# VectorE's expert steps 2 to 13 as one hardware loop, with the first tile's closing norm moved behind the last step

## What is computed

```
v1, i1 = lax.top_k(s1, K)
v2, i2 = lax.top_k(s2, K)
cand_s = (v1[..., :, None] + v2[..., None, :]).reshape(B, T, H, K * K)
cand_e = (i1[..., :, None] * PEER_N_KEYS + i2[..., None, :]).reshape(B, T, H, K * K)
top_s, top_pos = lax.top_k(cand_s, K)
experts = jnp.take_along_axis(cand_e, top_pos, axis=-1)
g = jax.nn.softmax(top_s, axis=-1)
...
u = expert_down[e].astype(f32)
hdn = jax.nn.gelu(jnp.einsum('chkd,cd->chk', u, xt.astype(f32)))
return jnp.einsum('chk,chkd->cd', gt * hdn, expert_up[e].astype(f32))
...
h = h + peer_ffn(rms_norm(h, norm2_g[layer]), ...)
return rms_norm(h, norm_f_g)
```

## Time and profile before

| what | value |
|---|---|
| median of 3 runs | 871.92 us (871.73 to 872.32) |
| the profiled execution's own time | 871.49 us |
| its span in the profile | 869.8 us |
| busy: PE, DVE, ACT, POOL | 753.9, 563.8, 177.5, 580.4 us |
| gathers (queue q0) | 268.47 MB, 77.7% of 16 engines' span |
| HBM read | 306.93 MB |

### The profile page before, as it was taken

The page is one execution under the profiler, slowest core; times in us unless marked ns, Lnnn a source line. Parts: engine busy times, 40 slices in busy tenths (PEclk is TensorE's granted clock), DMA queues, the critical chain, the costliest instruction groups (busy, mean ns, idle before and its releaser), DMA issues.

```text
span 869.8 us, 9153 instructions
## 1 busy us (share of the span) xinstructions
PE 753.9 (87%) x2453; PEld 388.7 (45%) x2453; DVE 563.8 (65%) x1501; ACT 177.5 (20%) x557; POOL 580.4 (67%) x718
## 2 busy tenths in 40 slices
PE   8999999999997979788888888787878797777786
PEld 5988768556552424244333434242434342222232
DVE  2554686239998667676667676676666676765534
ACT  1134455211212021122202030203020211102010
POOL 5886551017777777777777777777777777777760
PEclk9999999999999999999999999999999999999999
DMA  8858460669999999999999999999999999999995
GB/s 291 224 149 221 156 253 2 233 250 359 398 410 383 411 408 410 410 410 409 409 409 409 409 409 410 409 410 408 410 409 410 410 409 410 409 410 411 410 409 230
DMA packets 99619, 308.94 MB, mean 355 GB/s; under 512 B 18512, under 2 KB 23424, under 8 KB 99584
## 3 DMA queue, kind: packets, MB, share of 16 engines
q0 software_dynamic: 73728, 268.47, 77.7%
q1 hardware_dynamic: 24784, 39.91, 13.8%
q10 hardware_dynamic: 1072, 0.16, 0.1%
HBM read 306.93 MB, written 1.05 MB: 354 GB/s over the span
## 4 chain that ended last, share of the span: by engine, by line
DMA 31%; PE 27%; POOL 23%; issue 11%; DVE 7%; ACT 1%; POOLq 0%; ACTq 0%; DVEq 0%
PE bank L1526 23%; DMA region_w<-in_expert_up,chosen 19%; POOL region_w L643 17%; DMA region_w<-in_expert_down,chosen 5%; DMA dn_spare<-in_expert_down,chosen 4%; POOL gates L643 3%; DMA pool_bd<-in_expert_down,chosen 3%; PE xn_ps L1526 2%; PE bank L1529 2%; DVE region_w L1382 2%; POOL pool_bd L643 1%; POOL dn_spare L643 1%; DVE gates L1382 1%; DVE pool_bd L1382 0%; DMA hvrep<-in_norm_g 0%
## 5 line engine op out<-in xcount | busy, mean ns | idle before, releaser
L1526 PE MATMUL bank<-region_w,pool_bd 128*128 128x512 f32 (+2 forms) x1004 | 472.6, 598 | 102.1 <-DMA region_w<-in_expert_up,chosen 99.8
L1526 PEld LDWEIGHTS bank<-region_w,pool_bd 128*128 128x128 f32 x1004 | 174.0, 189 | 372.7 <-issue 297.2
L643 POOL DMA_INDIRECT region_w<-in_expert_up,chosen x250 | 237.7, 951 | 81.3 <-issue 60.9
L1382 DVE CUSTOM_DVE_ANT_0 region_w<-xn_ps,region_w 128x1024 f32<-128x1024 f32 x128 | 156.5, 1224 | 101.4 <-DMA region_w<-in_expert_down,chosen 101.0
L643 POOL DMA_INDIRECT region_w<-in_expert_down,chosen x128 | 121.2, 947 | 40.5 <-issue 33.2
L1382 DVE CUSTOM_DVE_ANT_0 gates<-xn_ps,gates 128x1024 f32<-128x1024 f32 x64 | 78.1, 1223 | 36.2 <-DMA gates<-in_expert_down,chosen 34.1
L906 ACT ACTIVATE pool_bd<-ident,pool_bd 128x128 f32<-128x128 f32 x250 | 78.5, 389 | 80.7 <-PE bank L1526 59.8
L643 POOL DMA_INDIRECT gates<-in_expert_down,chosen x64 | 61.1, 955 | 23.4 <-issue 17.4
L709 ACT ACTIVATE pool_bd<-bank 128x256 f32<-128x256 f32 (+3 forms) x49 | 19.0, 389 | 267.1 <-PE bank L1526 242.9
L1382 DVE CUSTOM_DVE_ANT_0 dn_spare<-xn_ps,dn_spare 128x1024 f32<-128x1024 f32 x32 | 39.2, 1224 | 24.0 <-DMA dn_spare<-in_expert_down,chosen 23.9
L1526 PE MATMUL bank<-region_q,oT 128*128 (+1 forms) x240 | 54.3, 379 | 0.0
(11 more groups left out here) (285 smaller groups left out, 782.2 us busy)
## 6 DMA issues: line engine op xcount, KB each, us to landing
region_q<-in_w_in SPq DMA_DIRECT2D x4, 2048.0 KB, 8.8
region_q<-in_w_query SPq DMA_DIRECT2D x1, 6144.0 KB, 22.6
region_w<-in_expert_up,chosen POOLq DMA_INDIRECT x250, 14.4
region_w<-in_w_out SPq DMA_DIRECT2D x1, 3072.0 KB, 21.0
x_sb<-in_x SPq DMA_DIRECT2D x4, 512.0 KB, 4.1
region_q<-in_w_in SPq DMA_DIRECT2D x2, 1024.0 KB, 10.7
region_q<-in_w_in SPq DMA_DIRECT2D x16, 128.0 KB, 3.0
region_w<-in_wb_nsa SPq DMA_DIRECT2D x2, 1024.0 KB, 16.4
```

Of the source, the lines that this page charges most:

```text
L643: pool.indirect_dma_start(out=row, out_offset=None, in_=table, in_offset=bass.IndirectOffsetOnAxis(ap=of_slot(chosen, s, k), axis=0)).then ...
L1382: dve.tensor_tensor_reduce(out=row, in0=xn_ps[:, :], in1=row, scale=1.0, scalar=0.0, op0=ALU.mult, op1=ALU.add, accum_out=hdn[:, k:k + 1]) ...
L1526: return pe.matmul(out_, lhsT, rhs, start=start, stop=stop)
```

## The change

Three things are edited.

1. DVE: one loop runs turns 2 to 13. The number of the tile is now the loop's register shifted right by three, so the columns of `stat` (the per-token scales) are addressed by a register, and the wait for the second tile's tokens (`xn_in`) is in each turn, against a value worked out in a register. The wait for the scales (`rstd2`) in a turn is for 6 from the start, that is, for both tiles. The two `add_y(0, ...)` and `hy_ready` stand behind the loop, at step 14 in place of step 9, and `norm_f(0)` stands behind the coefficients of step 15.
2. ACT: its sum of squares moves from step 9 to step 13, behind that step's `softmax_exp`.
3. POOL: the 1/root moves from before up row 160 to before up row 240.

```diff
         def per_token(what, t):
-            return stat[:, what + t:what + t + 1]
+            return stat[:, bass.ds(what + t, 1)]
...
-                if n == 10 * SLOTS:
+                if n == LAST * SLOTS:
                     pool.wait_ge(ssq3, 1)
                     rstd(stat[:, 26:27], stat[:, 24:25], DM).then_inc(rstd3, 1)
...
-                if s == NH + 1:
-                    act.wait_ge(hy_ready, 1)
-                    act.activation(gt[:, 1, 0:DM], xs[:, 0, :], ACT.Square, accum_out=stat[:, 24:25]).then_inc(ssq3, 1)
                 if s + 2 < STEPS:
                     softmax_exp(s + 2)
...
+                if s == LAST - 2:
+                    act.wait_ge(hy_ready, 1)
+                    act.activation(gt[:, 1, 0:DM], xs[:, 0, :], ACT.Square, accum_out=stat[:, 24:25]).then_inc(ssq3, 1)
                 gelu_tanh(s + 1)
...
             def highest(p, t):
-                dve.wait_ge(rstd2, 3 * t + 3)
+                dve.wait_ge(rstd2, 6 if not isinstance(p, int) else 3 * t + 3)
...
-            def turn(s, t, t_next, t_choice):
-                picking = choose(s + 2, t_choice)
+            def turn(s):
+                picking = choose(s + 2, (s + 2) >> 3)
                 next(picking)
                 for k in range(SLOTS - AHEAD, SLOTS):
                     dot(k, s)
                     next(picking, None)
-                polynomial(s, t)
-                if t_next != t:
-                    dve.wait_ge(xn_in, 4)
-                begin(s + 1, t_next, picking)
+                polynomial(s, s >> 3)
+                dve.wait_ge(xn_in, 2 + 2 * ((s + 1) >> 3))
+                begin(s + 1, (s + 1) >> 3, picking)
...
-            turns(2, NH - 2, 0)
-            turn(NH - 2, 0, 0, 1)
-            turn(NH - 1, 0, 1, 1)
-            turn(NH, 1, 1, 1)
+            behind = own.n
+            with dve.Fori(2, LAST - 1) as i:
+                own.turn = (i - 2) * OWN_TURN
+                turn(i)
+            own.turn, own.n = 0, behind + OWN_TURN * (LAST - 3)
             dve.wait_ge(up_used, NH * SLOTS)
             own.mark(add_y(0, 0))
             own.mark(add_y(0, 1))
             own.wait()
             dve.engine_nop().then_inc(hy_ready, 1)
-            turns(NH + 1, LAST - 1, 1)
-            dve.wait_ge(gf_in, 16)
-            dve.wait_ge(rstd3, 1)
-            norm_f(0)
...
             polynomial(LAST, 1)
             coefficients(LAST)
+            dve.wait_ge(gf_in, 16)
+            dve.wait_ge(rstd3, 1)
+            norm_f(0)
```

More of the change, by code:

```diff
@@ L1465, in turn @@
                     next(picking, None)
-                polynomial(s, t)
-                if t_next != t:
-                    dve.wait_ge(xn_in, 4)
-                begin(s + 1, t_next, picking)
[L1471 to L1478, removed]
-            begin(2, 0, picking)
-            turns(2, NH - 2, 0)
-            turn(NH - 2, 0, 0, 1)
-            turn(NH - 1, 0, 1, 1)
-            turn(NH, 1, 1, 1)
+                polynomial(s, s >> 3)
+                dve.wait_ge(xn_in, 2 + 2 * ((s + 1) >> 3))
+                begin(s + 1, (s + 1) >> 3, picking)
+            begin(2, 0, picking)
+            behind = own.n
+            with dve.Fori(2, LAST - 1) as i:
+                own.turn = (i - 2) * OWN_TURN
+                turn(i)
+            assert own.n == behind + OWN_TURN, own.n - behind
+            own.turn, own.n = 0, behind + OWN_TURN * (LAST - 3)
             dve.wait_ge(up_used, NH * SLOTS)
```

## The result

The changed kernel takes 870.48 us (median of 12 runs, 869.26 to 871.22) where the kernel before takes 872.02 (12 runs, 870.7 to 873.56). The ratio is 0.9981, with a 95% interval of 0.9974 to 0.9988: **1.5 us faster**, which is little, but the interval leaves out 1. Ten of the runs further down fell in a stretch in which every kernel, the one before too, took 956 to 973 us at a granted clock of 0.91 to 0.95 and with some 310 to 380 GB/s in windows of 40 us of the stage, and they are not compared with the others.

A forecast was written before the change was run, and what follows sets the result against it. The prediction took gather transfers at 409 GB/s to bound the expert stage. Every term came to 0, the write as -1.19 + 1.19, so 871.49 + 0 for the profiled execution, 871.9 us for the median, range 871.0 to 873.1.

The forecast's parts named there:

- What bounds the kernel: Expert stage: gathers fill each 41 us step at 409 GB/s; issue delays under about 11.5 us leave the transfers fed.
- the signs: Windows below 409 GB/s, dot 9's wait ended by issue instead of transfer, or L1409 waiting for `rstd3` would disprove the prediction.
- The program gets shorter: Rival: some unseen fetch or start gets cheaper; 15 instruction packets are 0.4 us of transfers, so 871.5 at the least.
- Turns in the loop: Turns 6, 7 and 8 on DVE: register work up to 5.1 us in total, covered by DVE's spare time; cost 0.
- the loop's edge: Dot 9, first work behind each edge, waits for its row anyway; three more edges cost 0.
- fetches at the edges: Case of instruction fetches at the loop's edges, given a chance of 0.02.
- Adds, norm, square, 1/root: Adds and norm on DVE, square on ACT: cost 0 each; 1/root on POOL: 0 to 0.8 us, taken as 0.
- The write: SP's 512 KB write of the first tile moves from 780 to about 838 us: -1.19 + 1.19 = 0.
- The rival of the hidden write: The late write finds free transfer time behind the last gather issue: 870.7 us, chance 0.05.
- The chances: For the whole kernel: faster 0.02, within 0.2% 0.93, slower 0.05.
- the gain of more than 1.7 us: Case of the whole kernel getting over 1.7 us faster for something no row shows, chance 0.02.
- no change: Main case for the whole kernel: all parts sum to 0, median 871.9 us, chance 0.88.

The follow-up runs named there:

- the program written out: The changed kernel with its 12 turns written out in place of the loop: 876.27 us, ratio 1.0046 to the kernel before.
- the norm alone: The kernel before with only the square, the 1/root, the norm and the first tile's write late: 872.22 us, ratio 1.0004 to the kernel before.
- more_rows: The changed kernel with 48 SP writes of one 4 KB row, one every four gathers, to the stage's end: 876.0 us, ratio 1.0045 to the kernel before.
- the run with one row: The changed kernel with 16 SP writes of one 4 KB row each in steps 3 to 8: 871.04 us, ratio 0.9984 to the kernel before.

## Why the prediction was wrong

- *What bounds the kernel* was right: transfers fill the stage before and after, at the same GB/s. Wrong was the sentence drawn from it, that "what moves no bytes moves no end". What a dot waits for is the last of a gather's 16 landings, in the kernel before up to 1.75 us behind the 15th (724 to 740 us), and the table of windows shows the mean of 16 engines, at 409 to 410 GB/s in both kernels. None of the signs that the prediction named for its being wrong appeared, since it named none that could show one engine.
- *The program gets shorter* is the step that failed. It saw the cause and priced it by bytes: 15 packets of instructions, 0.4 us of transfers in all. Measured: 0.8 to 1.0 us for one fetch of VectorE once its engine has no lead, three of them gone, 2.1 us together in the profile with the small step behind 511.5. The forecast let this case begin at 871.5; with 2.1 in its place the forecast would have been 869.8, and the 0.7 from there to the 870.48 measured are of the size of the start and the write in the balance above, but no run takes them apart. The packets stood in the earlier trace rows; their times in the stage, and the dots 2 us behind each, were never laid side by side.
- *Turns in the loop, the loop's edge*: right. The new loop, 12 turns in place of nine in two, keeps its dots at 2.56 us and its waits at 1.3. The 0.02 that the forecast gives to fetches at the edges was my estimate, and no run shows such a fetch: the changed kernel has fewer packets (8 on q14 for 11), not one more for each turn, none comes with the loop's turns (three on q14 in the more than seven turns between the two dots), and the program written out was the slower one, by 876.27 - 870.65 = 5.6 us.
- *Adds, norm, square, 1/root*: right, all hidden. L936 ran at 776.6, L1409 at 835.58 without a wait, and the pair on POOL ahead of up row 240 left the gathers in order:

```profile
822.25 0.18 POOL L535 TENSOR_SCALAR stat<-stat 128x1 f32<-128x1 f32 x1
822.52 0.57 POOL L536 TENSOR_TENSOR stat<-stat 128x1 f32<-128x1 f32 x1
823.28 1.01 POOL L643 DMA_INDIRECT dn_spare<-in_expert_up,chosen  x1 [0.18 <-issue]
```

- *The write*: right, -1.19 at 780 and 0.8 to 1.4 back at the end; alone it measured +0.16 us, with 0 inside its interval.
- *The rival of the hidden write*: it would have given 870.7, near the 870.48 measured, but that is not what happened: the norm alone, which has that write, gained nothing.
- *The chances*: 1.5 us are inside the 0.2% that had 0.93, and the gain of more than 1.7 us, at 0.02, did not come. But the time is not "no change", which had 0.88, and a small gain from fewer fetches had no chance of its own and no place in the range: a lower end of 871.0 was too high for a change that took some 30% of an engine's program away in a stage with no free transfer time.

## What to carry to other kernels

Where transfers fill a stage, look at the packets of instructions in the queues and at when they come: here each fetch of VectorE's program lay on one DMA engine, and it cost up to 1 us of the whole stage, 50 times what its bytes say. A loop was faster here than the same turns written out, with its register work under cover. Judge a one-row transfer in such a stage by the time of one engine (0.15 us a write here, its packet 0.16), not by a sixteenth, once the engine's lead is used up, and read the pace of landings from the instructions that wait for them; the mean of GB/s hardly showed it here (436 to 750 us: 409 before, 410 changed, 410 with `more_rows`).

## What was not expected of the hardware

- A fetch of 8 KB has a packet of 0.34 us but puts the landings back by 0.96. The write of 4 KB has one of 0.16 and costs 0.15. What fills the other 0.6 us of a fetch (work of the engine that has no record, or a wait inside it) stays open.
- Not every fetch costs. The changed kernel has three packets on q14 and one of 16 KB on q8 between 436 and 750 us and keeps the pace. I take them for those of other engines, an estimate: VectorE is in its loop there for more than seven turns, and no step of the dots stands behind them. The landing records of the kernel before show two such packets on an engine with a lead: behind those at 742.1 and 759.0 the last landing is only 1.12 us behind the 15th instead of 1.75, but still 4.28 behind the first, so another engine fell back and the dots lost nothing.
- The level at which the stage settles differs between executions: dot 4 of step 3 stood at 312.55 us before, at 313.21 in the changed kernel, at 314.17 in the run with one row, which does nothing else until then. Whether the kernel before settles earlier by rule is open, with one profile of it; it may be why the two profiled executions differ by 1.0 us where the medians differ by 1.5.
